# The first block's mixers and output projection in one stage, each mixer's outputs turned and split behind its own gate

## The chip, the cores and the metric

The kernel runs on one core of a Trainium2 chip. The metric is the device time of one execution in microseconds (us). Lower is better.

## What is computed

Two network blocks run over 512 tokens of width 1024, in fp32. The change touches only the first, which has two layers. Each layer projects the tokens, runs four different sequence mixers on 256 columns each, multiplies their joined outputs by `w_out`, and adds and normalises:

```python
for l in range(DEPTH):                       # DEPTH = 2
    p = jnp.einsum('btd,dc->btc', h, w_in[l])
    pa, pb, pc, pd = _split(p, MIXER_COLS)
    ya = _hgrn2_mixer(pa, ...)               # 256 columns each
    yb = _gla_mixer(pb, ...)
    yc, v_first = _rwkv7_mixer(pc, v_first, ...)
    yd = _retnet_mixer(pd, positions, log_gamma)
    mix = jnp.einsum('btc,cd->btd', jnp.concatenate([ya, yb, yc, yd], axis=-1), w_out[l])
    h = _layer_norm(DN_ALPHA * h + mix, ln1_g[l], ln1_b[l])
    ...                                      # layer 0: dense SwiGLU; layer 1: 8 experts, 2 per token
```

Each mixer ends with a norm over the 64 columns of every head, then a product with a gate.

## The kernel before

Every stage is a `Block`: five instruction streams, written out by hand, one for each engine (PE is the matmul engine, ACT the scalar engine, DVE the vector engine, POOL the general one; SP only issues transfers). A stream runs strictly in the order written, and waits on semaphores. A block ends when all of its streams have ended, so nothing of the next stage starts earlier.

The part that matters here is three such stages in each layer:

1. `stage_mixers` (L2660). The four mixers are objects: E (retention), H (hgrn), L (gla), R (rwkv). Their steps are interleaved by hand in each stream. The tail of DVE's list is, in order: `H.dve_scale`, `L.dve_update(6)`, `R.dve_centre` (L244 and on), `H.dve_gate`, `L.dve_state(0)` (L343), `L.dve_out(0)`, `R.dve_variance`, `L.dve_state(1)`, `L.dve_out(1)`, `R.dve_scale`, `L.dve_state(2)`, `L.dve_out(2)`, `R.dve_extra` (L1327), `L.dve_out(3)` (L366), `R.dve_gate` (L277), `L.dve_variance`, `L.dve_scale`, `L.dve_gate` (L277). A gate writes the mixer's 256 columns of `Y`, which is token-major (512 tokens by 1024, four tiles of 128 tokens). E is gated long before that tail, H at its start, then R, and L last. On PE the last work is `L.pe_out(c)` (L320, L324) and `L.pe_state(c)` (L333), token tile by token tile; `L.pe_turn` (L304) needs what ACT took in `L.act_take(5)` and `(6)` (L505).
2. `stage_to_feature` (L2394). PE turns all of `Y` to feature-major with 32 transposes of 128 by 128 (L2410). For each of the eight tiles of 128 features, ACT copies the rounded part from PSUM (`hi`, L2418), and DVE subtracts it from the original to get the rest (`lo`, L2429). SP loads the first two pieces of `w_out` meanwhile (L2444).
3. `stage_out` (L2929). `w_out` comes in four pieces of 1 MB: piece p holds 512 feature rows by 512 columns; pieces 0 and 1 make up the first column half, with feature tiles 0 to 3 and 4 to 7. Each is split like the outputs: ACT copies `hi` (L3020), DVE makes `lo` (L3046). A product is three matmuls of 128x512 (hi·hi, hi·lo, lo·hi), so a piece and a token tile take 12 matmuls, and a column half 96 (L2966). After the first half, DVE adds the residual (L3050); in the second half, tile by tile, it adds, normalises (L3060 to L3070), PE turns the tile again (L2977), and ACT and DVE split it for the next stage (L3030, L3042). In layer 0, the first weight unit of the next stage is also split here (L216, L222); in layer 1 the router's products run here (L2985) and the first expert weights are loaded.

In feature tiles, H owns 0 and 1, L owns 2 and 3, R owns 4 and 5, E owns 6 and 7.

## Time and profile before

| what | us |
|---|---|
| median of 3 runs | 3019.81 |
| lowest and highest of them | 3019.56, 3030.49 |
| the profiled execution, its own time | 3009.14 |
| its span, first to last instruction | 3007.3 |
| PE busy in the span | 2765.7 |

The profiled execution lies below all three timed runs. A row of a busy-time view shows a stretch in us from the start of the span, its length, then for each engine (PE, its weight loads PEld, DVE, ACT, POOL) the busy us and the number of instructions in brackets, then the TensorE clock that was granted (1.00 is 2.4 GHz, 0.50 is 1.2 GHz, what lies between is a mean of the two), the busy share of the transfer engines, and GB/s. A row of a timeline shows start, length, engine, line of the kernel, operation, what it writes and reads, how many instructions of that kind were merged, and in square brackets how long the engine was idle before and what released it. "PEq" as a releaser is PE's sequencer, which stands here for the end of the block before. SPq rows are transfers being issued.

### The profile page before, as it was taken

To read this page: it belongs to the slowest core of one execution; us is meant where nothing else is said; L and a number is where in the kernel's file an instruction comes from. 1 tells how busy PE (TensorE), PEld (TensorE's weight loads), DVE (VectorE), ACT (ScalarE), POOL (GpSimd) and SP (SyncE) were. 2 spreads that over 40 slices of the span, in tenths; PEclk is the share of its full clock that TensorE was granted. 3 is DMA by queue.
4 is the path that set the end of the run, shared out by engine and by line. 5 is a ranking of instruction groups with operands and counts; after the bars stand their busy time and mean duration, and the time that the engine had idled before them with its cause. 6 is when DMAs were issued, how large, how long until landed. Compare 5 with 4: busy or idle time off the path is not lost. (4 is left out here: it accounts for less than half of the span.)

```text
span 3007.3 us, 38431 instructions
## 1 busy us (share of the span) xinstructions
PE 2765.7 (92%) x14780; PEld 2365.6 (79%) x14780; DVE 1543.4 (51%) x2136; ACT 1085.4 (36%) x1524; POOL 205.8 (7%) x205
## 2 busy tenths in 40 slices
PE   7999989999999999869999999949999897899999
PEld 5779867878877798658888888848878775788787
DVE  3526664233445366547777777763232525732333
ACT  2334223222233241225555555532222416431222
POOL 0011200000000112050000000110000002000000
PEclk9999989999999999879999999979999996899999
DMA  4310034152222100338888888953242210251521
GB/s 151 94 56 1 1 98 123 49 147 75 84 87 84 45 1 1 113 108 246 240 236 234 230 236 238 265 149 98 67 126 84 67 49 20 84 140 49 147 67 67
DMA packets 435565, 335.24 MB, mean 111 GB/s; under 512 B 23488, under 2 KB 375744, under 8 KB 435312
## 3 DMA queue, kind: packets, MB, share of 16 engines
q1 hardware_dynamic: 429360, 318.14, 36.7%
q0 software_dynamic: 3008, 10.09, 1.0%
q10 hardware_dynamic: 3072, 5.24, 0.5%
q8 instruction: 90, 1.47, 0.2%
q14 instruction: 35, 0.29, 0.0%
HBM read 323.43 MB, written 9.99 MB: 111 GB/s over the span
## 5 line engine op out<-in xcount | busy, mean ns | idle before, releaser
L2197 PE MATMUL psum<-x_split,gate_up_split 128*128 128x512 f32 x1056 | 415.5, 393 | 13.4 <-DVE h_tok L2307 5.3
L2198 PE MATMUL psum<-x_split,gate_up_split 128*128 128x512 f32 x1056 | 414.1, 392 | 0.0
L2199 PE MATMUL psum<-x_split,gate_up_split 128*128 128x512 f32 x1056 | 414.0, 392 | 0.0
L3400 PE MATMUL psum<-x_slots_split,gate_up_split 128*128 128x320 f32 x1424 | 381.1, 346 | 16.1 <-DVE gate_up_split L3621 12.6
L3401 PE MATMUL psum<-x_slots_split,gate_up_split 128*128 128x160 f32 x1424 | 316.0, 242 | 0.0
L2320 DVE TENSOR_TENSOR arena<-arena,psum 128x512 f32<-128x512 f32 x66 | 45.4, 688 | 515.3 <-ACT arena L2262 515.3
L2530 PE MATMUL psum<-x_split,w_split 128*128 128x512 f32 x1152 | 272.3, 396 | 11.7 <-DVE w_split L2567 6.5
L3400 PEld LDWEIGHTS psum<-x_slots_split,gate_up_split 128*128 128x128 f32 x1424 | 262.7, 190 | 24.3 <-issue 22.2
L2530 PEld LDWEIGHTS psum<-x_split,w_split 128*128 128x128 f32 x1152 | 217.3, 190 | 66.7 <-issue 15.0
L3401 PEld LDWEIGHTS psum<-x_slots_split,gate_up_split 128*128 128x128 f32 x1424 | 266.2, 192 | 1.9
L2262 ACT ACTIVATE arena<-psum 128x512 f32<-128x512 f32 x66 | 39.5, 598 | 622.8 <-PE psum L2199 622.8
L2197 PEld LDWEIGHTS psum<-x_split,gate_up_split 128*128 128x128 f32 x1056 | 200.5, 190 | 57.1 <-issue 15.5
L2198 PEld LDWEIGHTS psum<-x_split,gate_up_split 128*128 128x128 f32 x1056 | 200.8, 190 | 41.7
L2199 PEld LDWEIGHTS psum<-x_split,gate_up_split 128*128 128x128 f32 x1056 | 200.2, 190 | 42.3
L3621 DVE TENSOR_TENSOR gate_up_split<-arena,gate_up_split 128x2048 fp32r<-128x2048 f32 x88 | 200.9, 2284 | 0.0
L2292 DVE TENSOR_TENSOR gate_up_split<-arena,gate_up_split 128x2048 fp32r<-128x2048 f32 x63 | 144.2, 2292 | 74.2 <-ACT gate_up_split L2243 74.2
L2216 PE MATMUL psum<-down_split,hidden_split 128*128 128x512 f32 x432 | 168.6, 390 | 1.0 <-DVE hidden_split L2322 1.0
L2218 PE MATMUL psum<-down_split,hidden_split 128*128 128x512 f32 x432 | 168.1, 389 | 0.0
L2217 PE MATMUL psum<-down_split,hidden_split 128*128 128x512 f32 x432 | 168.1, 389 | 0.0
L3554 ACT ACTIVATE gate_up_split<-arena 128x2048 fp32r<-128x2048 f32 x88 | 167.3, 1902 | 1.0 <-DMA arena<-in_moe_w_up 1.0
L3626 DVE TENSOR_TENSOR down_split<-arena,down_split 128x512 fp32r<-128x512 f32 x176 | 121.1, 692 | 71.1 <-ACT down_split L3560 70.4
L2530 PE MATMUL psum<-w_split,x_split 128*128 128x512 f32 (+1 forms) x672 | 143.0, 374 | 2.1 <-PE psum L2530 2.1
(515 smaller groups left out, 4690.6 us busy)
## 6 DMA issues: line engine op xcount, KB each, us to landing
arena<-in_moe_w_gate SPq DMA_DIRECT2D x91, 512.0 KB, 4.2
arena<-in_moe_w_up SPq DMA_DIRECT2D x91, 512.0 KB, 5.6
arena<-in_moe_w_down SPq DMA_DIRECT2D x176, 256.0 KB, 5.1
arena<-in_ffn_w_gu SPq DMA_DIRECT2D x88, 512.0 KB, 5.3
arena<-in_w_in SPq DMA_DIRECT2D x32, 1024.0 KB, 5.3
arena<-in_ffn_w_down SPq DMA_DIRECT2D x108, 256.0 KB, 5.2
arena<-in_ffn_w_gate SPq DMA_DIRECT2D x22, 512.0 KB, 4.1
arena<-in_ffn_w_up SPq DMA_DIRECT2D x22, 512.0 KB, 5.5
```

The source lines that it names most:

```text
L2197: nc.tensor.matmul(out, w[0], XR[:, 0, k, :], start=k == 0, stop=False)
L2198: nc.tensor.matmul(out, w[0], XR[:, 1, k, :], start=False, stop=False)
L2199: mm = nc.tensor.matmul(out, w[1], XR[:, 0, k, :], start=False, stop=k == DT - 1)
L2216: nc.tensor.matmul(out, x[0], w[0], start=f == 0, stop=False)
L2217: nc.tensor.matmul(out, x[0], w[1], start=False, stop=False)
L2218: mm = nc.tensor.matmul(out, x[1], w[0], start=False, stop=f == FU - 1)
L2292: nc.vector.tensor_tensor(GSPL[:, r, 1, :], GRAW[:, r, :], GSPL[:, r, 0, :].bitcast(F32), ALU.subtract).then_inc(*g_lo.up())
L2530: mm = nc.tensor.matmul(out, a, b, start=opens and k == 0 and q == 0, stop=closes and k == nk - 1 and q == 2)
L3400: hi = lambda start, stop: nc.tensor.matmul(out, wt[0], XE[:, k8, :, :].rearrange("p s n -> p (s n)"), start=start, stop=stop)
L3401: lo = lambda: nc.tensor.matmul(out[:, N:2 * N], wt[1], XE[:, k8, 0, :], start=False, stop=False)
L3554: nc.scalar.activation(GSPL[:, r, 0, :], GRAW[:, r, :], ACT.Copy).then_inc(g_hi.sem, 1)
L3621: nc.vector.tensor_tensor(GSPL[:, r, 1, :], GRAW[:, r, :], GSPL[:, r, 0, :].bitcast(F32), ALU.subtract).then_inc(g_lo.sem, 1)
```

## The change

`stage_to_feature` after the mixers and `stage_out` are gone. Their steps are a new class, `MixOut` (O), whose methods stand inside the streams of `stage_mixers`, so that one block does all three.

- The turn goes by mixer: `pe_group(m)` makes eight transposes (feature tiles 2m and 2m+1) as soon as that mixer is gated, `act_group(m)` copies the two `hi` tiles, `dve_group(m)` makes the two `lo` tiles. The order is E, R, H, L.
- The pieces are taken in the order 1, 0, 2, 3. Piece 1 needs the feature tiles of R and E, piece 0 those of H and L.
- Pieces 1 and 0 are loaded while the mixers run, into room that H has finished with. Piece 1 is split before `R.dve_centre`, piece 0 between the groups of H and L. Pieces 2 and 3, the gain rows and the router are loaded after L is gated. The next stage's first weights wait for the products of piece 1.
- Some semaphores are merged in pairs to make room for the new ones; `MOST_SIGNALS` goes from 111 to 113.
- The products, the residual, the norm and the turn of the second half are as before. The rounding of the next stage's first unit (layer 0) now waits for the end of the first column half.

The core of the diff:

```diff
+class MixOut(Part):
+    ORDER = (1, 0, 2, 3)
+    GROUPS = (3, 2, 0, 1)
...
+    def sp_first_pieces(self):
+        sp, k = self.nc.sync, self.k
+        sp.wait_ge(*self.H.out_mm.at(TT))
+        k.load_piece(sp, self.w, OUT_PIECES, MIX_RAW1 - DT * PW, 1)
+        sp.wait_ge(*self.H.variance_then_gated.at(1))
+        k.load_piece(sp, self.w, OUT_PIECES, MIX_RAW0, 0)
+
+    def sp_later(self):
+        sp, k = self.nc.sync, self.k
+        sp.wait_ge(*self.L.variance_then_gated.at(2))
+        for p in range(PRAW, 4):
+            k.load_piece(sp, self.w, OUT_PIECES, OUT_RAW, p)
+        for r, to in zip(self.rows, (self.G, self.Bb)):
+            sp.dma_start(to, r.partition_broadcast(P)).then_inc(*self.rows_in.up(16))
...
+        sp.wait_ge(*self.used.at(1))
+        sp.wait_ge(*self.lo.at(self.nth(0)))
+        if self.early is not None:
+            self.early.sp_load()
+        if self.ahead is not None:
+            self.ahead(sp)
+
+    def pe_group(self, m):
+        nc = self.nc
+        nc.tensor.wait_ge(*self.group[m].variance_then_gated.at(2))
+        if m == 3:
+            nc.tensor.wait_ge(*self.R.o_ready.at(TT))
+        if m == 0:
+            nc.tensor.wait_ge(*self.moved.at(2))
+        if m == 1:
+            nc.tensor.wait_ge(*self.moved.at(4))
+        for b in range(2):
+            for t in range(TT):
+                mm = nc.tensor.transpose(self.group_bank(m, b)[:, t * P:(t + 1) * P], self.Y[:, t, (2 * m + b) * P:(2 * m + b + 1) * P], self.k.cf("ident"))
+            mm.then_inc(*self.turned.up())
+
+    def act_group(self, m):
+        nc, n = self.nc, 2 * self.GROUPS.index(m)
...
+        for b in range(2):
+            nc.scalar.wait_ge(*self.turned.at(n + b + 1))
+            nc.scalar.activation(self.k.XR[:, 0, 2 * m + b, :], self.group_bank(m, b), ACT.Copy).then_inc(*self.parts.up())
+
+    def dve_group(self, m):
+        nc, XR, n = self.nc, self.k.XR, 2 * self.GROUPS.index(m)
+        for b in range(2):
+            nc.vector.wait_ge(*self.parts.at(n + b + 1))
+            nc.vector.tensor_tensor(XR[:, 1, 2 * m + b, :], self.group_bank(m, b), XR[:, 0, 2 * m + b, :].bitcast(F32), ALU.subtract).then_inc(*self.moved.up())
+
+    def act_piece(self, p):
+        nc = self.nc
+        nc.scalar.wait_ge(*self.loaded[p % PRAW].at(16 * (p // PRAW + 1)))
+        if p == 1:
+            nc.scalar.wait_ge(*self.R.out_mm.at(TT))
+        if p == 0:
+            nc.scalar.wait_ge(*self.R.gate_ready.at(1))
+        nc.scalar.activation(self.k.WMIX[p][:, 0, :], self.raw[p], ACT.Copy).then_inc(*self.hi.up())
+
+    def dve_piece(self, p):
+        nc, W = self.nc, self.k.WMIX[p]
+        nc.vector.wait_ge(*self.hi.at(self.nth(p)))
+        nc.vector.tensor_tensor(W[:, 1, :], self.raw[p], W[:, 0, :].bitcast(F32), ALU.subtract).then_inc(*self.lo.up())
...
+    def pe_first_half(self):
+        nc, k = self.nc, self.k
+        self.pe_group(2)
+        self.pe_piece_ready(1)
+        nc.tensor.wait_ge(*self.moved.at(4))
+        for t in range(TT):
+            mm = self.pe_products(1, t, k.bank(t), True, False)
+            if t == 0:
+                self.pe_group(0)
+            if t == 2:
+                self.pe_group(1)
+        mm.then_inc(*self.used.up())
+        self.pe_piece_ready(0)
+        nc.tensor.wait_ge(*self.moved.at(8))
+        for t in range(TT):
+            self.pe_products(0, t, k.bank(t), False, True).then_inc(*self.products.up())
...
+    def act_second_half(self):
...
+        if self.early is not None:
+            nc.scalar.wait_ge(*self.products.at(TT))
+            self.early.act_round()
...
@@ stage_mixers, PE
                     if c < TT - 1:
                         L.pe_state(c)
+                    if c == TT - 2:
+                        O.pe_group(3)
+                O.pe_first_half()
+                O.pe_second_half()
@@ stage_mixers, ACT
                 R.act_scan_out(3)
+                O.act_piece(1)
                 L.act_take(5)
                 L.act_take(6)
                 L.act_diagonal()
                 L.act_turned()
                 R.act_square()
                 R.act_root()
+                O.act_piece(0)
+                O.act_group(3)
                 L.act_square()
+                O.act_group(2)
                 L.act_root()
+                O.act_group(0)
+                O.act_group(1)
+                O.act_second_half()
@@ stage_mixers, DVE
                 L.dve_update(6)
+                O.dve_piece(1)
                 R.dve_centre()
...
                 R.dve_extra()
+                O.dve_group(3)
                 L.dve_out(3)
                 R.dve_gate()
+                O.dve_group(2)
                 L.dve_variance()
                 L.dve_scale()
                 L.dve_gate()
+                O.dve_group(0)
+                O.dve_piece(0)
+                O.dve_group(1)
+                O.dve_first_half()
+                O.dve_second_half()
@@ block_one
-            self.stage_mixers(l)
-            self.stage_to_feature(Y, None, split=self.XR, ahead=self.first_pieces(ap["w_out"][l], OUT_PIECES, OUT_RAW))
...
-                self.stage_out(ap["w_out"][l], rows[0], rows[1], early=early)
+                self.stage_mixers(l, ap["w_out"][l], rows[0], rows[1], early=early)
```

## Rows read from the trace of the kernel before

**Rows 1.** The page, part 1: busy time, share of the span, instructions

```profile
PE 2765.7 (92%) x14780; PEld 2365.6 (79%) x14780; DVE 1543.4 (51%) x2136; ACT 1085.4 (36%) x1524; POOL 205.8 (7%) x205
```

**Rows 2.** Busy time by stretch, layer 0: engines, granted clock, DMA share, GB/s

```profile
394.00:400.60 6.60, 0.16 (x3) 0.05 (x2) 5.65 (x7) 1.27 (x2) 0.00 (x0) 0.64 0.00 0
400.60:408.80 8.20, 6.33 (x32) 6.09 (x32) 5.34 (x8) 4.62 (x8) 0.00 (x0) 0.67 0.73 256
408.80:413.20 4.40, 0.02 (x1) 0.05 (x1) 2.46 (x2) 3.71 (x2) 0.00 (x0) 0.57 0.73 234
413.20:436.50 23.30, 23.30 (x97) 19.14 (x97) 8.59 (x6) 5.64 (x3) 0.00 (x0) 0.93 0.64 182
```

**Rows 3.** The same view for the same three gaps of layer 1

```profile
1213.00:1219.80 6.80, 0.36 (x5) 0.25 (x3) 5.64 (x7) 1.27 (x2) 0.00 (x0) 0.65 0.00 0
1219.80:1228.00 8.20, 6.32 (x32) 6.08 (x32) 5.34 (x8) 4.63 (x9) 0.00 (x0) 0.67 0.71 257
1228.00:1232.40 4.40, 0.03 (x1) 0.06 (x1) 2.47 (x2) 3.70 (x2) 0.00 (x0) 0.57 0.56 226
```

**Rows 4.** Timeline of PE, layer 0: start, length, instructions, idle before, releaser

```profile
383.64 0.53 PE L304 MATMUL psum<-const_sb,arena 128*128 128x128 f32 x3
...
392.38 0.43 PE L324 MATMUL psum<-arena 128*128 128x64 f32 x2 [1.10 <-DVE arena L350]
```

**Rows 5.** Timeline of DVE, end of the mixers of layer 0

```profile
380.23 1.21 DVE L244 TENSOR_REDUCE small<-arena 128x16 f32<-128x1024 f32 x1
...
385.54 0.42 DVE L343 COPY arena<-psum 128x256 f32<-128x256 f32 x1 [1.50 <-PE psum L333]
...
394.25 0.43 DVE L366 TENSOR_TENSOR arena<-psum,arena 128x256 f32<-128x256 f32 x1 [0.46 <-DVE arena L1327]
394.59 1.21 DVE L277 TENSOR_TENSOR arena<-arena,psum 128x1024 f32<-128x1024 f32 x1
...
399.05 1.22 DVE L277 TENSOR_TENSOR arena<-arena 128x1024 f32<-128x1024 f32 x1
...
410.74 4.50 DVE L3046 TENSOR_TENSOR w_split<-arena,w_split 128x2048 fp32r<-128x2048 f32 x2 [2.24 <-ACT w_split L3020]
```

**Rows 6.** Timeline of ACT, the same stretch

```profile
376.52 1.18 ACT L505 ACTIVATE arena<-psum 32x512 f32<-32x512 f32 x2
...
408.80 3.71 ACT L3020 ACTIVATE w_split<-arena 128x2048 fp32r<-128x2048 f32 x2 [1.19 <-PEq L2400]
```

**Rows 7.** Timeline of all engines, start of the turn stage of layer 0

```profile
400.55 0.93 SPq L2444 DMA_DIRECT2D arena<-in_w_out  x2
```

**Rows 8.** Timeline of all engines, projection of layer 0

```profile
413.18 23.48 PE L2966 MATMUL psum<-w_split,x_split 128*128 128x512 f32 x96 [6.25 <-DVE w_split L3046]
...
418.27 1.92 ACT L3020 ACTIVATE w_split_out<-arena 128x2048 fp32r<-128x2048 f32 x1 [5.76 <-DMA arena<-in_w_out]
...
442.21 0.69 DVE L3060 SCALAR_TENSOR_TENSOR h_tok<-h_tok,psum 128x512 f32<-128x512 f32 x1 [0.25 <-PE psum L2966]
...
447.39 1.03 PE L2977 MATMUL psum<-const_sb,h_tok 128*128 128x128 f32 x8
...
448.02 1.09 ACT L3030 ACTIVATE x_split<-psum 128x512 fp32r<-128x512 f32 x2 [3.72 <-PE psum L2977]
```

**Rows 9.** Timeline of all engines, end of the projection stage of layer 0

```profile
464.36 1.94 PE L2977 MATMUL psum<-const_sb,h_tok 128*128 128x128 f32 x8 [3.21 <-DVE h_tok L3070]
...
465.48 0.60 ACT L3030 ACTIVATE x_split<-psum 128x512 fp32r<-128x512 f32 x1 [3.09 <-PE psum L2977]
...
466.97 0.69 DVE L3042 TENSOR_TENSOR x_split<-psum,x_split 128x512 fp32r<-128x512 f32 x1 [0.16 <-ACT x_split L3030]
```

**Rows 10.** Busy time by stretch: parts with a low and a full TensorE clock

```profile
413.20:416.30 3.10, 3.10 (x7) 2.43 (x8) 2.04 (x1) 0.00 (x0) 0.00 (x0) 0.50 0.68 183
416.30:436.50 20.20, 20.20 (x91) 16.71 (x89) 6.56 (x5) 5.64 (x3) 0.00 (x0) 1.00 0.64 182
400.60:406.00 5.40, 5.40 (x26) 5.40 (x27) 3.00 (x5) 3.01 (x6) 0.00 (x0) 0.50 0.79 267
```

More of the change, by code:

```diff
@@ L66 @@
 OWN_MU = 96
-MOST_SIGNALS = 111
+MOST_SIGNALS = 113
 LASTING = ("moe_", "ffn_gate_up_loaded", "w_piece_loaded")
@@ L233, in norm @@
         self.o3, self.sq3 = flat(O), flat(SQ)
-        self.squared, self.var_ready, self.root_ready = (self.sig(n) for n in ("outputs_squared", "head_variance_ready", "head_root_ready"))
+        self.squared_then_root, self.variance_then_gated = (self.sig(n) for n in ("outputs_squared_then_head_roots", "head_variances_then_gated_outputs"))
         if center:
@@ L253, in act_square @@
             nc.scalar.wait_ge(*self.o_ready.at(TT))
-        nc.scalar.activation(self.SQ, self.O, ACT.Square).then_inc(*self.squared.up())
+        nc.scalar.activation(self.SQ, self.O, ACT.Square).then_inc(*self.squared_then_root.up())
     def dve_variance(self):
         nc, s = self.nc, self.dve
-        nc.vector.wait_ge(*self.squared.at(1))
+        nc.vector.wait_ge(*self.squared_then_root.at(1))
         s.link(nc.vector.tensor_reduce(self.var, self.sq3, AX.X, ALU.add))
-        nc.vector.tensor_scalar(self.var, self.var, 1.0 / HD, self.eps, ALU.mult, ALU.add).then_inc(*self.var_ready.up())
+        nc.vector.tensor_scalar(self.var, self.var, 1.0 / HD, self.eps, ALU.mult, ALU.add).then_inc(*self.variance_then_gated.up())
     def act_root(self):
-        self.nc.scalar.wait_ge(*self.var_ready.at(1))
-        self.nc.scalar.activation(self.var, self.var, ACT.Sqrt).then_inc(*self.root_ready.up())
+        self.nc.scalar.wait_ge(*self.variance_then_gated.at(1))
+        self.nc.scalar.activation(self.var, self.var, ACT.Sqrt).then_inc(*self.squared_then_root.up())
     def dve_scale(self):
         nc, s = self.nc, self.dve
-        nc.vector.wait_ge(*self.root_ready.at(1))
+        nc.vector.wait_ge(*self.squared_then_root.at(2))
         s.link(nc.vector.reciprocal(self.var, self.var))
@@ L276, in dve_gate @@
         nc.vector.wait_ge(*self.gate_ready.at(1))
-        self.dve(nc.vector.tensor_tensor(self.out, self.O, self.gate, ALU.mult))
+        self.dve.wait()
+        nc.vector.tensor_tensor(self.out, self.O, self.gate, ALU.mult).then_inc(*self.variance_then_gated.up())
 class Linear(HeadNorm):
@@ L2031, in __init__ @@
         self.WEARLY = place("w_split_early", 2 * DT * PW, EARLY_SPL, F32R).rearrange("p (s n) -> p s n", s=2)
+        self.WMIX = [place("w_split_mix", 2 * DT * PW, MIX_W0, F32R).rearrange("p (s n) -> p s n", s=2), self.WSPL[2], self.WSPL[0], self.WSPL[1]]
         self.HIDS = place("hidden_slots_split", 2 * FU * CAP, HIDS0, F32R).rearrange("p (f n) -> p f n", f=FU)
@@ L2658, in row, with stage_mixers @@
         return self.area(FT0 - D + i * GROUP, GROUP)
-    def stage_mixers(self, l):
+    def stage_mixers(self, l, w, row_g, row_b, early=None, ahead=None, router=None):
         nc = self.nc
@@ L2667, in stage_mixers @@
         R = Rwkv(self, l)
-        top = LEVELS - 1
+        O = MixOut(self, w, row_g, row_b, (R, L, H, E), early, ahead, router)
         with nc.Block() as block:
@@ L2676, in _ @@
                 sp.wait_ge(*E.loaded.at(48))
+                O.sp_first_pieces()
+                O.sp_later()
             @block.gpsimd
@@ L2875, in _ @@
                 L.dve_log()
-                E.dve.wait()
+                dve.wait_ge(*E.variance_then_gated.at(2))
                 R.dve_solve_u(6)
@@ L2911, in _ @@
                 L.dve_state(0)
-                H.dve.wait()
+                dve.wait_ge(*H.variance_then_gated.at(2))
                 L.dve_out(0)
@@ L3195, in block_one @@
                 gwm, uwm, dwm = ap["moe_w_gate"][0], ap["moe_w_up"][0], ap["moe_w_down"][0]
-                self.stage_out(ap["w_out"][l], rows[5], rows[6], ahead=self.first_units(gwm[0], uwm[0], "moe", FRING), router=ap["moe_router"][0])
+                self.stage_mixers(l, ap["w_out"][l], rows[5], rows[6], ahead=self.first_units(gwm[0], uwm[0], "moe", FRING), router=ap["moe_router"][0])
                 self.stage_router()
```

274 lines of the change are left out of this document (136 added, 138 removed).

## The prediction

> **What bounds the kernel now.** I read the page's busy times first: PE is busy for 2765.7 us of a span of 3007.3 [rows 1]. So only time in which PE stands still, or runs at its low clock, can be won by reordering. Next I read the busy times by stretch, cut where the stages meet. In layer 0 PE has almost nothing to do for 6.60 us while DVE and ACT finish R and L, then turns for 8.20 us, of which 6.33 are 32 transposes, and then stands for 4.40 us while the first weight piece is split [rows 2]. Together these are 19.2 us between the last mixer product and the first projection product, with 6.5 us of PE work in them. Layer 1 repeats it: 6.80, 8.20 and 4.40 [rows 3]. The projection that follows keeps PE busy for all of its first half, 23.30 us [rows 2]. So I look for the time at which the first projection product can start, 413.18 now [rows 8], and for what is added to PE after it. The rest of the kernel should follow at its old distance.
>
> **The tail of the mixers gets longer.** Numbers are for layer 0, one layer at a time.
> - Piece 1 is split on DVE before `R.dve_centre`: two such splits take 4.50 us, so one costs 2.25 [rows 5]. DVE stands idle for 1.50 us before 385.54, waiting for PE [rows 5]; that absorbs 1.50, and 0.75 is left as delay. Its ACT copy (1.9 us [rows 8]) goes ahead of L's two takes; the first starts at 376.52 [rows 6] and both would end by about 381, while PE asks for them at 383.64 [rows 4]. I cost it at nothing; without that cover it is 1.9 us.
> - The turn of E: PE's eight transposes take 1.03 us [rows 8], and PE has 1.10 us idle at that place [rows 4]. On DVE two rests of 0.69 [rows 9] make 1.38, of which an idle 0.46 [rows 5] is used up. Delay now 0.75 + 0.92 = 1.67 us. What queues behind it is `L.dve_out(3)` and R's gate, which ends at 394.59 + 1.21 + 1.67 = 397.47 instead of 395.80 [rows 5].
> - The turn of R is now the chain that releases PE: transposes, ACT, DVE. No row shows it at this place. The nearest are the last turn of the projection stage, at a low clock, from 464.36 to 466.97 + 0.69, 3.30 us [rows 9], and an earlier one at full clock, whose ACT copies end 0.63 + 1.09 us after the start, plus 0.69 on DVE, 2.41 us [rows 8]. PE has idled before it and the clock had a mean of 0.64 in this stretch [rows 2], so I take 3.30. The first product starts at 400.77, 12.41 us earlier. At the other end it would be 399.88.
> - ACT does E's copies and piece 0 in time in which it waited; it was busy for 1.27 us of these 6.60 [rows 2].
>
> **What is added behind that start.** The turns of H and L stand inside the product stream: 2 x 1.03 = 2.06 us of PE [rows 8]; at the low clock H's would be 1.94 instead of 1.03 [rows 9]. The 96 products themselves are the same. Net gain 12.41 - 2.06 = 10.35 us a layer.
>
> **Is anything else late then?** L's four DVE steps took 399.05 + 1.22 - 395.80 = 4.47 us after R's gate [rows 5], and start at 400.77: L is gated at 405.24. H's rests (1.38) and piece 0 (2.25) follow, to 408.9. PE asks for L after three tiles: with 2.91 us a tile (23.30 / 8) that is 400.77 + 8.73 + 1.03 = 410.5. L's rests are done 2.41 later, at 412.9, and PE needs them after its fourth tile, at 410.5 + 1.03 + 2.91 = 414.5. So 1.6 us are spare. Pieces 2 and 3 and the gain rows are moved behind L's gate on SP. The pair issued at 400.55 [rows 7] was in use by 408.80 [rows 6], when the block before had ended, so landing takes at most 8.3 us: by 413.6. Two splits on top, 4.50, end near 420 at worst, behind L's rests too; the second half begins at 400.77 + 2.06 + 23.30 = 426.1. The next stage's first weights are issued when piece 1's products end, 414.5, and land by 422.8. In the second half DVE is 0.25 us ahead of PE [rows 8]. The rounding of the next unit, now behind the first half's products, takes 1.92 us as an equal copy does [rows 8], beside DVE's last add and its statistics; I cost it at nothing, with 1.9 us in layer 0 as the other end. The early loads run in a stretch without other transfers.
>
> **The clock.** The first 3.10 us of the projection were granted 0.50: 7 products there, against 91 in the 20.20 us behind it, 0.222 each [rows 10]. That cost 3.10 - 7 x 0.222 = 1.55 us, and the turn stage ran 5.40 us at 0.50 before the clock rose [rows 10]. After the change PE idles for less time before the projection, but has a short burst and a short gap in it. The low clock may last between 0 and 5.4 us, so its cost lies between 0 and 2.7, against 1.55 now. I take the same 1.55, since the nearest row is the same products after a similar gap.
> The Trainium skill ("TensorE: Matmul & The Clock Gate", "What's actually happening") says that activity releases the throttle, that idling brings it back, and that the same kernel meets a different number of slow matmuls from run to run. By the row the term is zero; by the page it could be anything between a gain of 1.55 and a loss of 1.15 a layer. The two layers here both began slow, and no run here shows the other case.
>
> **The sum.** Two layers of 10.35 us are 20.7 us. The profiled execution's own time was 3009.14, its span 3007.3; with this it would be 2988.4. The timed runs are 3019.56, 3019.81 and 3030.49, so the profiled one lies 10.7 below their median. I subtract from the median: 3019.81 - 20.7 = 2999.1 us.
> Ends for a layer: 10.35 + 0.89 (R's turn at full clock) + 1.55 (no low clock) = 12.8, and 10.35 - 1.15 (long low clock) - 0.91 (H's turn at it) - 1.0 (half of the unseen 1.9) = 7.3. That gives 2994 to 3005 from the median.
>
> **Rivals.**
> - DVE's tail doesn't absorb what is put in. The idle times of 1.50 and 0.46 are waits for PE, and PE waits for DVE's states in turn, so the loop may slide as a whole. Then 1.96 us more a layer: 3003.0. For it: the last PE steps wait for DVE (1.10 at 392.38 [rows 4]). Against: DVE's wait at 385.54 ends by PE work that doesn't depend on the steps delayed.
> - A warm clock: the projection starts at full clock in both layers, 12.8 a layer: 2994.2. For it: E's turn and R's turn shorten PE's gaps. Against: in both layers the mean was already 0.64 and 0.65 in the 6.6 us after the last mixer product [rows 2, 3].
> - The overlap doesn't happen: PE's first product comes only when L is gated, because DVE works through L before R's rests or ACT is held up. Start at 405.24 instead of 400.77, 4.47 us less a layer: 3008.1, no measurable change. Against: the order on DVE puts R's rests ahead of L's variance, and ACT is nearly idle.
> - Slower: the broken-up stream holds the low clock through the projection's first half. A product at the low clock takes 3.10 / 7 = 0.443 us [rows 10], 0.221 more, so 96 cost 21.2 us, 19.7 more than the 1.55 now. Net loss 9.3 us a layer: 3038. It decides when the low clock lasts some 24 us (3.1 + 10.35 / 0.5) instead of 3.1. Against: in a dense stream it rose after 3.10 us [rows 10].
>
> **Chances.** Forecast 0.62, sliding tail 0.14, warm clock 0.12, no overlap 0.07, slower 0.03, something that I don't see 0.02. The range holds the first three with the bounds of a layer; it reaches down to 2985, because runs of the same kernel lie at 3009 as well as 3020, and 20.7 below 3009.14 is 2988.4. Its upper end is 3006. A measurement of this kernel can tell about 0.5%, 15.1 us, from no change. The first three cases lie below 3004.7 but for their upper ends, so faster 0.84; no overlap and those ends, 0.12; slower 0.04.
>
> **What would show it.** In the timeline of the new kernel: R's gate ends 1.5 to 2 us later than before; the first projection product starts 12 to 13 us earlier; no gap in PE's 96 products but the two turns, with the second half's first product about 10.4 us earlier; from there the same distances as before. A wait of PE for DVE before piece 0's products would show that the 1.6 us spare are gone. I am wrong if the first product starts after L's gate, if the stretch from there to the second half is over 28 us, or if a later stage takes back what these two won.

## The result, and the profile after

The changed kernel takes 3013.97 us, the median of 18 runs (3002.6 to 3022.21), beside 3022.94 for the kernel before in 18 runs (3013.4 to 3040.98). The ratio is 0.9957, with a 95% interval of 0.9941 to 0.9974: 13.0 us or 0.43% less, between 7.9 and 17.8. (The two medians lie only 9.0 us apart, the means of the same runs, 3025.9 and 3012.7, 13.2.) I had forecast 2999.1 us and a gain of 20.7. The sign is right; the time lies above the range that I gave, and the gain lies within the 0.5% that I had called no change, though its interval doesn't reach 1.

The profiled execution of the changed kernel took 3002.6 us (span 3000.8, mean granted clock 0.950). First the page's busy times, which stand against [rows 1]:

```profile
PE 2778.2 (93%) x14780; PEld 2374.6 (79%) x14780; DVE 1542.7 (51%) x2136; ACT 1085.3 (36%) x1524; POOL 208.7 (7%) x205
```

The instruction counts are the same, and yet PE is busy for 12.5 us longer. That is the first sign that more of the same work was done at the low clock. Next, PE's timeline in layer 0, from L's last level to the second half of the projection (start, length, instructions, idle before and what ended it); it answers to [rows 4] and [rows 8]:

```profile
374.29 1.95 PE L468 MATMUL psum<-arena 128*128 128x256 f32 x8
...
385.30 0.43 PE L328 MATMUL psum<-arena 128*128 128x64 f32 x2 [1.38 <-DVE arena L347]
...
392.46 1.77 PE L2069 MATMUL psum<-const_sb,arena 128*128 128x128 f32 x8
...
397.60 1.97 PE L2069 MATMUL psum<-const_sb,arena 128*128 128x128 f32 x8 [1.65 <-DVE arena L281]
401.07 4.44 PE L2106 MATMUL psum<-w_split,x_split 128*128 128x512 f32 x12 [1.50 <-DVE x_split L2084]
405.35 1.04 PE L2069 MATMUL psum<-const_sb,arena 128*128 128x128 f32 x8
406.14 5.74 PE L2106 MATMUL psum<-w_split,x_split 128*128 128x512 f32 x24
411.72 1.03 PE L2069 MATMUL psum<-const_sb,arena 128*128 128x128 f32 x8
412.51 3.02 PE L2106 MATMUL psum<-w_split,x_split 128*128 128x512 f32 x12
415.36 11.04 PE L2106 MATMUL psum<-w_split_mix,x_split 128*128 128x512 f32 x48
```

The four turns are the L2069 lines: E, R, H, L. The first product starts at 401.07, and from there PE has no gap up to 426.2. DVE's timeline of the same stretch (against [rows 5] and [rows 8]) has piece 1 at 378.48, R's gate at 396.33, R's rests at 399.38, L's gate at 404.19, and the first residual add of the second half at 431.95 instead of 442.21:

```profile
378.48 2.28 DVE L2098 TENSOR_TENSOR w_split<-arena,w_split 128x2048 fp32r<-128x2048 f32 x1
...
396.33 1.21 DVE L281 TENSOR_TENSOR arena<-arena,psum 128x1024 f32<-128x1024 f32 x1
...
399.38 0.69 DVE L2084 TENSOR_TENSOR x_split<-psum,x_split 128x512 fp32r<-128x512 f32 x1 [1.84 <-ACT x_split L2078]
...
404.19 1.23 DVE L281 TENSOR_TENSOR arena<-arena 128x1024 f32<-128x1024 f32 x1
...
431.95 0.69 DVE L2218 SCALAR_TENSOR_TENSOR h_tok<-h_tok,psum 128x512 f32<-128x512 f32 x1 [0.25 <-PE psum L2106]
```

What the clock did is seen in the busy times by stretch (as in [rows 2]; the column before the last two is the granted clock). Layer 0:

```profile
383.90:387.20 3.30, 1.92 (x16) 1.86 (x16) 2.97 (x5) 0.81 (x3) 2.62 (x3) 0.99 0.02 5
387.20:393.90 6.70, 6.45 (x27) 5.84 (x26) 4.56 (x8) 2.04 (x2) 0.00 (x0) 0.50 0.00 0
393.90:397.30 3.40, 2.06 (x19) 1.92 (x17) 3.37 (x5) 1.76 (x3) 0.00 (x0) 0.99 0.00 0
397.30:404.20 6.90, 5.10 (x16) 4.05 (x17) 4.42 (x8) 1.61 (x4) 0.00 (x0) 0.51 0.00 0
404.20:426.20 22.00, 22.00 (x106) 18.36 (x105) 12.45 (x11) 5.78 (x6) 0.00 (x0) 1.00 0.77 239
```

and layer 1, where [rows 3] had the same picture as layer 0:

```profile
1196.00:1203.00 7.00, 7.00 (x28) 4.14 (x28) 6.04 (x8) 4.25 (x5) 0.00 (x0) 0.99 0.00 0
1203.00:1219.90 16.90, 16.45 (x70) 15.43 (x71) 11.67 (x18) 4.83 (x7) 3.62 (x4) 0.50 0.00 1
1223.30:1230.20 6.90, 5.40 (x17) 4.05 (x15) 5.38 (x7) 1.41 (x3) 0.00 (x0) 0.51 0.00 0
```

In the profile of before the low level lay around PE's waits and on the turn stage. Here it lies on L's last steps, 6.45 busy us of 6.70 in layer 0 and 16.45 of 16.90 in layer 1, and again on R's turn and the first products.

To compare kernels I count from the start of L's last level (374.29 above, 376.04 before), in microseconds, and cut the rest of the profile at stages whose code is the same in both. "Tail" is the stretch from that level to the first residual add of the second half; "mixers" is what comes before it in the same stage.

| profile | R's gate ends, layer 0 / 1 | first product | tail | mixers | projection in front of layer 1's mixers | span |
|---|---|---|---|---|---|---|
| before | 19.8 / 19.8 | 37.1 / 37.1 | 66.2 / 66.2 | 165.4 / 165.4 | 186.4 | 3007.3 |
| after | 23.3 / 26.8 | 26.8 / 29.8 | 57.7 / 61.3 | 165.7 / 175.2 | 187.0 | 3000.8 |

The tails are 8.5 and 4.9 us shorter. The mixers of layer 1, with the same work in them, took 9.8 us longer. With what lies between (-2.0 us up to the first mixers, +0.3 in them, +0.6 and +0.6 behind, -2.3 at the end) that is the 6.5 us between the two spans.

### The profile page after: what moved, and what is told of

It is laid out like the page before. It is cut to its first block and busy times, and to the rows that moved or that the text cites. A ratio compares the mean times of both kernels' runs of the same rounds, so it can differ in the third digit from the quotient of the medians.

```text
span 3000.8 us, 38408 instructions
## 1 busy us (share of the span) xinstructions
PE 2778.2 (93%) x14780; PEld 2374.6 (79%) x14780; DVE 1542.7 (51%) x2136; ACT 1085.3 (36%) x1524; POOL 208.7 (7%) x205
## 5 line engine op out<-in xcount | busy, mean ns | idle before, releaser
L3510 PEld LDWEIGHTS psum<-x_slots_split,gate_up_split 128*128 128x128 f32 x1424 | 260.7, 189 | 25.2 <-issue 23.0
L2438 PEld LDWEIGHTS psum<-x_split,gate_up_split 128*128 128x128 f32 x1056 | 201.0, 190 | 57.7 <-issue 15.9
L3664 ACT ACTIVATE gate_up_split<-arena 128x2048 fp32r<-128x2048 f32 x88 | 167.3, 1902 | 0.9 <-DMA arena<-in_moe_w_up 0.9
```

The lines of the kernel that those rows point to most:

```text
L2438: nc.tensor.matmul(out, w[0], XR[:, 0, k, :], start=k == 0, stop=False)
L3510: hi = lambda start, stop: nc.tensor.matmul(out, wt[0], XE[:, k8, :, :].rearrange("p s n -> p (s n)"), start=start, stop=stop)
L3664: nc.scalar.activation(GSPL[:, r, 0, :], GRAW[:, r, :], ACT.Copy).then_inc(g_hi.sem, 1)
```

## The experiments

**The changed kernel again** (no edit), to see a second profile and more times.

> The changed kernel once more, unaltered, for a second profile. Theory A (the delay put into DVE's tail lengthens PE's waits there, the granted clock falls inside the mixers' tail, and L's last steps run at 1.2 GHz): the clock is low again for several us before R's gate in both layers, the first projection product starts 7 to 10.5 us earlier than in the kernel before, and the second half of the products 5 to 8.5 us earlier; ratio to before 0.995 to 0.997. Theory B (that fall was chance, the kernel before has it as often): another pattern, at least one layer without a low clock before R's gate, its first product over 12 us earlier.

Median 3010.2 us, ratio 0.9972 (0.9945 to 0.9998). The two layers changed places: in layer 0 R's gate ended at +26.8, in layer 1 at +21.6. The clock in layer 1 stayed full up to the start of R's gate (1.00 in the first 13.0 us, and 0.94 in the 8.6 behind them), so this layer can be held against the kernel before at the same clock. PE there:

```profile
1212.06 0.43 PE L328 MATMUL psum<-arena 128*128 128x64 f32 x2 [1.38 <-DVE arena L347]
...
1222.66 1.97 PE L2069 MATMUL psum<-const_sb,arena 128*128 128x128 f32 x8 [2.47 <-DVE arena L281]
1226.14 5.46 PE L2106 MATMUL psum<-w_split,x_split 128*128 128x512 f32 x12 [1.50 <-DVE x_split L2084]
```

R's gate is 1.80 us later than in [rows 5] (1.67 forecast), the first product 12.06 earlier (12.41), and the tail 57.1 instead of 66.2: 9.1 us won, against 10.35. Most of what is missing is in the last line: 12 products take 5.46 us, where 12 at full clock take 3.02 and the first 12 of the kernel before took 4.44.

**Piece 1 split in R's turn.** Its rest on DVE moves behind R's gate, where DVE waits for the turn of R.

```diff
                 L.dve_update(6)
-                O.dve_piece(1)
                 R.dve_centre()
...
                 R.dve_gate()
+                O.dve_piece(1)
                 O.dve_group(2)
```

> The rest of piece 1 on DVE is moved from ahead of R's centring to behind R's gate, where DVE waited 1.84 us for the turn of R. Theory A: R's centring is back at its old place, PE's wait before L's second output is about 0.4 us again instead of 1.4, no low clock in the mixers' tail; the first product starts 1.5 to 2 us earlier than in the changed kernel in layer 0 and 4 to 5 earlier in layer 1, in all 5 to 7 us less: ratio to before 0.993 to 0.994. Theory B: only the direct 0.75 us a layer are won, 1.5 us in all, ratio 0.995 to 0.9955, and the clock may fall all the same.

Median 3006.26 us, ratio 0.9951 (0.992 to 0.9981). R's gate ends at +20.5 in both layers, 1.0 us sooner than in the changed kernel at full clock, and the tails are 56.2 and 56.1. PE, layer 0:

```profile
380.81 0.43 PE L328 MATMUL psum<-arena 128*128 128x64 f32 x2 [0.35 <-DVE arena L347]
...
391.42 1.97 PE L2069 MATMUL psum<-const_sb,arena 128*128 128x128 f32 x8 [2.47 <-DVE arena L281]
394.91 5.46 PE L2106 MATMUL psum<-w_split,x_split 128*128 128x512 f32 x12 [1.52 <-DVE x_split L2084]
```

PE's wait ahead of L's second output is 0.35 instead of 1.38 us, so that 1.0 us was piece 1's delay, close to the 0.75 worked out. What is left of the 1.80, 0.77, is E's turn, which I had put at 0.92. In the time it can't be told from the changed kernel. The low clock behind R's gate stayed.

**PE kept busy in its waits.** 33 transposes of a constant into a bank that nothing reads fill PE's waits in the tail and around R's turn; the output is the same.

```diff
                 if h == 0:
+                    if self.name == "gla":
+                        self.k.keep_warm(8 if c == 1 else 2 if c == 2 else 0)
                     nc.tensor.wait_ge(*self.z_ready.at(c))
...
         nc, k = self.nc, self.k
+        k.keep_warm(13)
         self.pe_group(2)
+        k.keep_warm(10)
         self.pe_piece_ready(1)
...
+    def keep_warm(self, n):
+        for _ in range(n):
+            self.nc.tensor.transpose(self.bank(1)[:, 0:P], self.cf("ident"), self.cf("ident"))
```

> The changed kernel with transposes of a constant into an unused PSUM bank where PE waited: 8 and 2 before L's second and third output, 13 before the turn of R and 10 behind it. If waits of PE bring the clock down (theory A): granted clock 1.00 from the mixers' tail into the projection, the first twelve products take 2.8 us instead of 4.4 to 5.1, and the sum is 3 to 9 us less than the changed kernel: ratio 0.993 to 0.9945. If the clock falls for other reasons (theory B): the clock is low as often as before, and the extra transposes cost 0 to 2 us a layer: ratio 0.996 to 0.997.

Median 2996.43 us, ratio 0.9902 (0.9874 to 0.9931): the best kernel here, ahead of both. PE, layer 0 (this kernel's lines lie two further down):

```profile
384.50 0.43 PE L330 MATMUL psum<-arena 128*128 128x64 f32 x2 [0.50 <-DVE arena L349]
...
392.47 1.59 PE L2326 MATMUL psum<-const_sb 128*128 128x128 f32 x13
395.10 1.09 PE L2071 MATMUL psum<-const_sb,arena 128*128 128x128 f32 x8 [1.04 <-DVE arena L281]
396.03 1.25 PE L2326 MATMUL psum<-const_sb 128*128 128x128 f32 x10
397.86 2.97 PE L2108 MATMUL psum<-w_split,x_split 128*128 128x512 f32 x12 [0.57 <-DVE x_split L2086]
```

R's turn takes PE 1.09 us instead of 1.97, and the first 12 products 2.97 instead of 4.44 to 5.46. The tails are 53.7 and 56.2. Busy times from L's last level to the first products of layer 0 show the full clock throughout:

```profile
373.50:398.00 24.50, 21.98 (x149) 17.86 (x149) 21.23 (x30) 11.23 (x15) 4.18 (x4) 1.00 0.00 1
```

In layer 1 the clock was low for 6.8 us of the tail, from 1198.7 on, and full behind that.

**All turns behind L's gate.** The weight pieces are still split early, but the hand-off by mixer is undone.

```diff
         nc, k = self.nc, self.k
+        nc.tensor.wait_ge(*self.L.variance_then_gated.at(2))
+        self.pe_group(3)
         self.pe_group(2)
...
-                    if c == TT - 2:
-                        O.pe_group(3)
                 O.pe_first_half()
...
                 L.dve_gate()
+                O.dve_group(3)
+                O.dve_group(2)
                 O.dve_group(0)
```

(and the same move on ACT, behind L's root).

> The turn by mixer is undone: all four turns, E R H L, stand behind L's gate, with the products of piece 1 behind the turns of E and R; the pieces are still split beforehand and it is still one stage. This leaves 'weights split beforehand' alone. L's gate ends 3 to 4 us earlier than in the changed kernel, but the first product comes about 4.5 us behind it: 3 to 6 us later than in the changed kernel in each layer, 6 to 12 us in all, ratio to before 0.998 to 1.000. If the turn by mixer were worth nothing, the ratio would be that of the changed kernel, 0.9957.

Median 3021.45 us, ratio 0.9998 (0.9972 to 1.0024): the gain is gone. The mean of its 12 runs is 3020.5 us, that of the changed kernel's 12 beside them (`again`) 3012.2. PE, layer 0:

```profile
407.40 3.67 PE L2069 MATMUL psum<-const_sb,arena 128*128 128x128 f32 x16 [6.27 <-DVE arena L281]
412.58 2.04 PE L2106 MATMUL psum<-w_split,x_split 128*128 128x512 f32 x4 [1.50 <-DVE x_split L2084]
```

The first products come at +33.7 and +30.6, where [rows 8] has +37.1, and the tails of this profile are 64.5 and 61.7. These look like a gain of some 6 us beside 66.2 twice, and none was measured; the mixers and the projection of the same profile (168.7 and 177.3, 188.6) were longer by more than that. So a tail's length alone, in one profile, says little of the time.

**The kernel before again** (no edit). I had put the low clock in the tail down to the change: more work of other engines between PE's steps. If so, a second profile of before would have none there.

> The kernel before once more, unaltered, for a second profile of its tail. If the kernel before keeps the clock high up to R's gate (theory A: the low clock there came with the change), both layers show 19.8 us from the start of L's last level to the end of R's gate again, and the first product 37.1 us behind that start. If it is as prone to the low clock (theory B), at least one layer shows 2 us or more in addition.

It took 3036.89 us (span 3035.1, clock 0.942). Busy times by stretch, layer 0:

```profile
378.30:386.00 7.70, 7.70 (x35) 4.84 (x34) 6.67 (x10) 2.46 (x4) 0.00 (x0) 1.00 0.00 1
386.00:400.00 14.00, 13.24 (x55) 12.14 (x54) 6.94 (x13) 1.83 (x4) 2.32 (x4) 0.50 0.01 2
400.00:413.40 13.40, 6.96 (x34) 6.80 (x34) 8.53 (x12) 3.66 (x6) 0.00 (x0) 0.50 0.23 76
```

and two lines of PE:

```profile
409.02 5.77 PE L2410 MATMUL psum<-const_sb,arena 128*128 128x128 f32 x32 [6.44 <-PEq L2669]
...
421.31 4.18 PE L2966 MATMUL psum<-w_split,x_split 128*128 128x512 f32 x9 [6.52 <-DVE w_split L3046]
```

The kernel before has it too, from 386.0 to 413.4. R's gate ends at +26.0 and +26.6 instead of +19.8, the tails are 73.3 and 73.0 instead of 66.2, and layer 1's mixers take 175.3 us, not 165.4. So that theory fell: the profile that I had predicted from was of an execution in which the low clock had come only behind R's gate, and had missed the last steps of L in both tails. That the longer mixers are the clock as well is seen in their busy times, layer 1, in the first profile of before:

```profile
1029.80:1195.20 165.40, 151.58 (x1242) 142.84 (x1243) 107.26 (x165) 58.68 (x89) 43.62 (x36) 0.96 0.03 9
```

and in the second, where the same 1242 matmuls keep PE busy for 10.15 us more, at 0.89 instead of 0.96, and DVE, ACT and POOL do what they did:

```profile
1039.90:1215.20 175.30, 161.73 (x1242) 151.93 (x1243) 107.24 (x165) 59.00 (x89) 43.64 (x36) 0.89 0.03 8
```

**Both edits, piece in the wait and transposes** (16 and 10 around R's turn, none at c == 1, 2 at c == 2).

> Both edits together: the rest of piece 1 behind R's gate, and transposes of a constant into an unused bank in PE's waits (2 before L's third output, 16 before and 10 behind the turn of R). Theory A: the gains are of different kinds and add, about 1 us a layer on top of the run with the transposes alone: product 23.3 to 23.6 us behind L's last level, ratio to before 0.989 to 0.990. If a shorter tail and the transposes win the same thing, the ratio stays at that of the transposes alone, 0.990 to 0.991, or is worse, since fewer transposes stand in the tail.

Median 2998.22 us, ratio 0.9905 (0.987 to 0.9939), no better than the transposes alone. The low clock met both tails (R's gate at +26.8, first product at +30.3 instead of the 23.3 to 23.6 expected, tails 59.7 twice), yet the stretch from the first product to the second half's add is 29.4 us, as in the kernel with transposes, instead of 30.9 to 32.3.

**Transposes in the kernel before**: 30 behind L's last output, 20 ahead of the first product of the projection.

```diff
                         L.pe_state(c)
+                self.keep_warm(30)
...
+                self.keep_warm(20)
                 for p in range(2):
```

> The kernel before with transposes of a constant in its own two gaps: 30 behind L's last output, 20 before the first projection product. Theory A (the clock is what limits both kernels here): the turn stage runs at 2.4 GHz and is then held by ACT and DVE, some 2 us less, and the first products save 1.55, in all 3 to 4 us a layer, 6 to 8 us: ratio 0.997 to 0.998. If the transposes were worth as much here as in the changed kernel (some 16 us), the ratio would be 0.9945; if nothing, 1.000 or slightly above.

Median 3027.14 us, ratio 1.001 (0.9985 to 1.0035). PE, layer 1:

```profile
1224.47 5.35 PE L2083 MATMUL psum<-const_sb 128*128 128x128 f32 x30
1231.12 3.68 PE L2416 MATMUL psum<-const_sb,arena 128*128 128x128 f32 x32 [1.31 <-PEq L2675]
1237.62 3.57 PE L2083 MATMUL psum<-const_sb 128*128 128x128 f32 x20 [2.81 <-PEq L2406]
1241.98 1.62 PE L2973 MATMUL psum<-w_split,x_split 128*128 128x512 f32 x3 [0.79 <-DVE w_split L3054]
```

The 32 turns take 3.68 us at full clock instead of 5.77 at the low one, and little comes of it: the first product still waits for the weight rests on DVE, and starts at +36.9 instead of +37.1. In layer 0, where L's last steps had met the low clock, it starts at +42.4, against +43.1 in the second profile of before. The tails are 70.0 and 66.0. What was expected here was a ratio of 0.997 to 0.998.

**Pieces split behind L's gate.** The other half undone: turns by mixer stay, pieces 1 and 0 are split last on ACT and DVE (SP loads pieces 2 and 3 behind them).

```diff
-                O.act_piece(1)
                 L.act_take(5)
...
-                O.act_piece(0)
                 O.act_group(3)
...
                 L.act_root()
+                O.act_piece(1)
                 O.act_group(0)
+                O.act_piece(0)
                 O.act_group(1)
...
                 L.dve_update(6)
-                O.dve_piece(1)
...
                 L.dve_gate()
+                O.dve_piece(1)
                 O.dve_group(0)
```

> The weights are not split beforehand: ACT copies and DVE's rests of pieces 1 and 0 stand behind L's last steps, where they stood before; the turn by mixer stays, and it is still one stage. R's gate ends 1 us earlier than in the changed kernel, but PE's first product waits for the rest of piece 1, which is done 2.3 us behind L's gate: about 4 to 6 us later than in the changed kernel a layer, 8 to 12 us in all, ratio to before 0.998 to 1.000. If the split beforehand were worth nothing, the ratio would be 0.996.

Median 3017.52 us, ratio 0.9995 (0.9966 to 1.0025). PE, layer 1:

```profile
1223.29 1.97 PE L2070 MATMUL psum<-const_sb,arena 128*128 128x128 f32 x8 [2.48 <-DVE arena L281]
1233.40 2.90 PE L2107 MATMUL psum<-w_split,x_split 128*128 128x512 f32 x6 [8.14 <-DVE w_split L2099]
```

R's turn is there early, and the product waits 8.14 us for the weight piece. With either half undone the gain in time is gone, as far as this can be measured.

**More profiles of the same kernels** (before, after, and after with the 33 transposes), to know what the tails do on most executions.

> The kernel before, unaltered, for one more profile. From the start of L's last level to the first residual add of the second half its two profiles so far showed 66.2 us a layer where the clock stayed high up to R's gate, and 73.0 to 73.3 where it was low. Theory B says that each layer is one or the other by chance: 66 or 73 again, or between. If the mean of the layers stays near 69.7, the changed kernel (57.1 to 61.3, mean 59.4) wins 10.3 us a layer there, as forecast, and what is missing is elsewhere.

> The kernel before, unaltered, once more: 66 or 73 us a layer, as in the other look, with a mean of 69 to 70 over all its layers. A mean under 67 would say that the kernel before keeps its clock more often than the changed one, and would explain the missing gain by itself.

> The changed kernel, unaltered, for one more profile. Theory B: each layer takes 57 us (high clock) or 61 us (low clock) over the same stretch. If what is missing from the forecast lies elsewhere, the stretch from layer 0's add to layer 1's last level is again 758 to 764 us, where the kernel before had 753 to 764, or the low clock outside these stretches is more than in the kernel before.

> The changed kernel, unaltered, timed beside the two that follow. Pooled with the two ratios so far (0.9957 and 0.9972) the mean should be 0.996: 0.995 to 0.997. A ratio near 0.993 would say that the forecast of 20.7 us was right and the first two timings were unlucky.

> The changed kernel with the transposes in PE's waits, for one more profile. If they keep the clock up, both layers take 53.7 to 56.3 us over the same stretch and the first twelve products 2.8 to 3.0 us. If that was chance, one layer is near 60 and its first twelve products take over 4 us.

The changed kernel's twelve runs (`again2`) had a median of 3006.21 us and a ratio of 0.9952 (0.9928 to 0.9976). The profiles, with those already told:

| profile | tails, layer 0 / 1 | mixers, layer 0 / 1 | projection in front of layer 1's mixers | span, clock |
|---|---|---|---|---|
| before | 66.2 / 66.2 | 165.4 / 165.4 | 186.4 | 3007.3, 0.952 |
| before, second | 73.3 / 73.0 | 167.3 / 175.3 | 186.8 | 3035.1, 0.942 |
| before, third | 73.3 / 73.1 | 170.3 / 175.2 | 187.0 | 3039.8, 0.942 |
| before, fourth | 73.3 / 73.0 | 167.3 / 175.2 | 187.0 | 3035.6, 0.941 |
| after | 57.7 / 61.3 | 165.7 / 175.2 | 187.0 | 3000.8, 0.950 |
| after, second | 61.3 / 57.1 | 171.3 / 167.3 | 188.8 | 3003.5, 0.949 |
| after, third | 61.1 / 63.6 | 167.4 / 171.9 | 189.0 | 3008.8, 0.947 |
| after, fourth | 61.2 / 62.1 | 175.2 / 173.7 | 188.8 | 3022.2, 0.942 |
| transposes | 53.7 / 56.2 | 162.4 / 173.7 | 188.7 | 2994.5, 0.954 |
| transposes, second | 56.3 / 53.8 | 174.4 / 165.4 | 186.6 | 2991.9, 0.955 |

Three of four profiles of before have tails of 73 us and one has 66.2. The mean tail is 71.4 us before (eight layers), 60.7 after, 55.0 with the transposes (four layers).

Four profiles are few, but the span and the mean clock of each timed run are on record too. In each kernel the span follows the mean clock closely, so a straight line through its runs gives the span at one and the same mean clock:

| kernel | timed runs | mean span | mean clock | span at a mean clock of 0.947, by the line |
|---|---|---|---|---|
| before | 86 | 3020.9 | 0.9474 | 3021.8 |
| after | 42 | 3009.4 | 0.9465 | 3008.4 |
| all turns behind L's gate | 12 | 3018.7 | 0.9447 | 3014.8 |
| pieces split behind L's gate | 12 | 3019.4 | 0.9453 | 3015.5 |

At the same mean clock the change is worth 13.4 us, and either half of it alone is worth 6 to 7. The two halves show no gain in time because their mean clock was lower. The transposes go the other way: their 11 runs have a mean clock of 0.9541 (0.951 to 0.959) and a mean span of 2993.5 us, and at equal clocks, 0.951 to 0.953, they took 2994.6 to 3000.6 us where the changed kernel took 2995.0 to 3002.9. So what they win is clock.

**The transposes, one place at a time**: those in the tail alone (8 and 2), and those around R's turn alone (13 and 10).

> The transposes of a constant only in PE's waits before L's second and third output (8 and 2), none around the turn of R. If the cost lies in the mixers' tail: most of the gain of the run with both, ratio 0.991 to 0.993, and R's gate ends 21.6 to 24 us behind L's last level, not 25 to 29. If it lies behind R's gate: the ratio is that of the changed kernel, 0.995 to 0.997, and the first twelve products still take 4.4 to 5.5 us.

> The transposes only behind L's last output (13) and behind the turn of R (10). If the cost lies behind R's gate: the first twelve products take 2.8 to 3.0 us, 1.3 to 2.7 less a layer, with R's turn 0.9 less: 4 to 7 us in all, ratio 0.993 to 0.995. If it lies in the tail: ratio 0.996, and R's gate ends as late as in the changed kernel in at least one layer.

Tail alone: median 3008.3 us, ratio 0.9952 (0.9924 to 0.998), R's gate at +21.6 and +25.7, stretch from the first product to the add 31.9 and 31.3. Around the turn alone: 3006.18 us, 0.9939 (0.9903 to 0.9974), R's gate at +26.8 twice, stretch 29.4 twice. So the 23 transposes around the turn are what repairs the start of the projection: 1.5 to 2.9 us a layer less than in the profiles of after (30.9 to 32.3). What those in the tail do for the clock there these layers can't say: with them R's gate was at +21.6, +24.1, +24.1 and +21.6 in the two profiles with both and at +21.6 and +25.7 here, at +26.8 in both layers without. Neither alone can be told from the changed kernel, whose own ratios were 0.9957, 0.9972 and 0.9952; together they can (0.9902, 0.9874 to 0.9931). The interval of those around the turn alone overlaps with this one, so that the ones in the tail add something is likely by the ratios, and not shown.

## Why the prediction was wrong, and where it was right

**PE's start is what counts: right.** The first product came 10.4 us sooner in layer 0 (+26.8 instead of +37.1) and 7.4 in layer 1, and the add of the second half followed it: 8.5 and 4.9 us sooner. Undoing either half of the change took the whole gain in time; at the same mean clock it took about half.

**The tail's delay: right at full clock.** 1.67 us were forecast and 1.80 measured where the clock was full. R's gate came 3.5 and 7.0 us later in the profile of after, but in the other three profiles of before, with the low clock there, it ends at +26.0 to +26.7, against +26.8 here. The sliding tail, 1.96 us more, is not borne out: what came on top was the clock.

**R's turn: right.** 3.30 us forecast from the gate to the first product; 3.53 in layer 0, 2.98 in layer 1, 2.81 with the transposes, where I had 2.41 for the full clock.

**The added turns: right.** The stretch from the first product to the add grew from 29.03 to 30.88 us in layer 0, by 1.85 where I had 2.06. By 2.46 it grew in layer 1, and by 2.99 in layer 1 of the second profile; there the clock comes in.

**The margins held.** PE went from piece 1 to piece 0 without a wait (415.36), so the 1.6 us spare were enough; the second half began 25.2 us behind the first product, under the 28 that I had named; the add waited the same 0.25 us for PE. No wait for a late load, and none for the copies moved on ACT, showed up in the stretch.

**The clock: the step that failed.** I wrote that I take "the same 1.55", so a net of nothing, with 1.15 more as the bad end, and counted it for the first products alone. Both were wrong. Twelve products that take 3.02 us took 4.44 to 5.46: 1.4 to 2.4 us, so 0.9 at most above the term. That part is small, and I had quoted the rule for it: the Trainium skill ("TensorE: Matmul & The Clock Gate", "What's actually happening") says that the number of slow matmuls varies from run to run, and the traces agree, with 4.44 to 5.46 us for the same twelve products in the profiles of one kernel. The larger part was outside the term: I had no term for the clock of the other stages. The low level reaches back into the mixers, where it adds 7 us to a tail of before and 4 us to one of after, and up to 10 us to the mixers ahead of it, in both kernels. In the tails alone this would make the gain larger, not smaller. What is taken back lies outside them: in the profile of after the tails win 8.5 and 4.9 us and the span only 6.5, and where both tails are at full clock they win 18.2, of which the timed runs show 13.4 at the same mean clock. I had drawn "the rest of the kernel should follow at its old distance" from one profile, whose span of 3007.3 us lies near the low end of this kernel's times.

**The sum again, with what the runs showed.** At the same full clock a layer gains 9.1 us (66.2 to 57.1); at the low one 73.3 to 61.2, some 12. Two layers: 18 to 24 us. From that go 1.6 us in layer 1's projection (186.8 before, 188.4 after, means of four profiles) and 0.6 behind the first tail. The 1.6 may be chance: layer 0's projection, which stands ahead of all changed code, differs by 1.4 the other way (185.7 before, 184.3 after). What is left, 16 to 22, is what the profiles show as well: the mean span of four is 3029.5 before and 3008.8 after.

The timed runs give less, 13.0 us with an interval up to 17.8, which holds the lower end of this and not the upper. That the profiles' means differ by the 20.7 of the forecast is luck in which executions were profiled: the four of before have a mean clock of 0.944 and a mean span 8.6 us above that of its 86 timed runs (0.9474), the four of after 0.947 and 0.6 us below (0.9465). The two kernels with half of the change undone fit this: their tails (64.5 and 61.7; 68.0 and 61.7) are shorter than 66.2 twice by some 6 and 3 us, they are 6 to 7 us faster at the same mean clock, and their lower clock takes it back. How often each kernel meets the low clock in its mixers can't be told from four profiles.

Layer 1's projection, with the same code, takes 186.4 to 187.0 us in all five profiles of the old stage and in four of the twelve of the new one, 188.6 to 189.1 in the other eight. The difference is the clock: PE is busy for 184.37 us of it at 0.98 in the second profile of after, for 181.95 at 0.99 in the first of before. The low stretch lies in the middle of it, some 69 us in. The busy times by stretch there, in the second profile of after:

```profile
912.90:918.90 6.00, 6.00 (x21) 2.81 (x22) 2.25 (x6) 3.07 (x3) 0.00 (x0) 0.72 0.29 99
```

and in the second of before, 68 us in:

```profile
921.20:927.20 6.00, 6.00 (x27) 3.97 (x27) 4.22 (x7) 2.69 (x3) 0.00 (x0) 1.00 0.21 70
```

Why it fell there, some 440 us behind the code that was changed, isn't settled.

Of the 14.9 us between the forecast and the median measured, 3.1 are a median of before of 3022.94 instead of 3019.81, 7.7 are the smaller gain (20.7 against 13.0), and 4.1 lie between the ratio, which compares runs made side by side, and the two medians.

**The rivals.** A warm clock in both layers (2994.2 us) was 19.8 off for the change as it is; the transposes give the first products the full clock in both layers, and then the median is 2996.43 and the ratio 0.9902. The slower case, a low clock throughout the first half, was the farthest off (3038) and didn't come near: after the first products the stream ran at 1.00. "No overlap", 3008.1 us, is the nearest in time, by another mechanism than the one that I gave for it: the overlap is there.

**A reason that I can only argue.** Before, PE had some 13 us without work in the tail of a layer [rows 2], and a low clock there cost nothing. The change fills these gaps, and the low clock is not shorter for it. As its measure take one less the mean clock, times the span, which is half the time at the low level: 0.048 x 3007.3 to 0.059 x 3035.6 = 144 to 179 us in the four profiles of before, 0.050 x 3000.8 to 0.058 x 3022.2 = 150 to 175 in those of after, and 159 as the mean over 86 timed runs of before and 161 over 42 of after. With fewer waits for it to fall into, more of it lies on work. An estimate of how much: in the profile of before the two waits of a layer hold 6.60 x 0.36 + 4.40 x 0.43 = 4.3 us of this measure [rows 2], 8.5 us in two layers; 20.7 less 8.5 is 12.2, near the 13.4 found at the same mean clock. The measure isn't a constant, though: it is 167 and 165 in the two kernels with half of the change undone, and 137 with the transposes. That transposes help after the change and do nothing before it (1.001, with the mean clock left at 0.9475) agrees with this, and doesn't prove it.

**Open.** Why the mean clock of a kernel is what it is, 0.9447 with the turns behind L's gate and 0.9541 with the transposes, isn't shown. In layer 1 of after the clock fell at 1203.0, behind 7.00 us in which PE was busy throughout, and in the second profile of before at 386.0 behind 7.70 such. In layer 0 of after it fell 1.9 us behind a wait of 1.38 us (385.30), and again around one of 1.65 (397.60). Why it fell in a full stretch isn't settled.

## What to carry to other kernels

- Handing work over in finer pieces pays where the next stage's engine starts sooner, and only if all its operands come sooner: here turned outputs or split weights alone gave nothing in time, and half at the same clock. Follow every operand of the first instruction of the new stage.
- Before one profile is used as the base of a sum, compare stage by stage with another profile of the same kernel. Here one stage of unchanged code differs by 10 us between two profiles, which is more than what the change gains in a layer. If each timed run has its mean clock beside it, compare two kernels at the same mean clock as well as by their medians: that parts the work saved from the clock.
- If TensorE's waits lie on the path and the next thing is its own work, harmless transposes in these waits can be worth as much as the reordering itself (0.9957 to 0.9902 here). Where it was another engine's work they were worth nothing (1.001).

## What the runs showed of the hardware

- TensorE's low level (granted 0.50, 1.2 GHz) lasted 27.4 us in one piece (386.0 to 413.4 in the second profile of before), 13.24 of its first 14.0 us with PE busy. I had known it only as 3 to 5 us after an idle stretch [rows 10].
- The span of a run follows the mean clock of the run in each kernel: in 42 timed runs of the changed one from 2995.0 us at 0.953 to 3020.3 at 0.941, by a straight line 2.3 us for each 0.001, and 2.65 in 86 runs of before.
- Ten transposes of 128x128 in f32 ahead of the first products, 1.25 us, together with 13 ahead of R's turn, kept these products at 2.97 to 3.01 us for twelve; without the 23 the twelve took 4.44 to 5.46.
